# Encoder trunk on one core: score products of 128 rows, scores ahead of a group's first transposes, weights loaded a phase early

## What is computed

```python
h = rmsnorm(x, norm_g)
proj = h @ w_in        # g_q g_k g_v g_lr z_a d_q d_k d_v z_b c_q z_c gate_in
o_a = gla_branch(g_q, g_k, g_v, g_lr, w2, b2, g_norm) * silu(z_a)
o_b = diff_attention(d_q, d_k, d_v, lam_params, g_norm) * silu(z_b)
o_c = memory_cross_attention(c_q, mem, ...) * silu(z_c)
merged = sum_i sigmoid(gate_in[i]) * (branch_i @ w_branch[i])
y = rmsnorm(x + merged @ w_out, final_norm_g)
# differential attention, 4 heads, two maps of 64 channels each:
s = einsum('ibhqd,ibhkd->ibhqk', qblk, kh) + bias     # i = 0, 1; bias = -slope * |tq - pos|
p = softmax(s);  a = p[0] - lam * p[1];  o = a @ v;  o = rmsnorm(o, g_norm) * (1 - lambda_init)
```

## Time and profile before

| | |
|---|---|
| median of 3 runs | 3633.05 us (3632.58 to 3635.64) |
| the profiled execution | 3617.7 us |
| its span | 3615.8 us |
| mean granted clock of TensorE | 0.974 of full |
| busy: TensorE, VectorE, ScalarE, GpSimd | 3411.0, 2048.2, 1326.5, 1213.1 us |
| DMA | 559.88 MB, mean 155 GB/s |

### The profile page before, as it was taken

The page is one execution under the profiler, slowest core; times in us unless marked ns, Lnnn a source line. Parts: engine busy times, 40 slices in busy tenths (PEclk is TensorE's granted clock), DMA queues, the critical chain, the costliest instruction groups (busy, mean ns, idle before and its releaser), DMA issues. The chain is left out here.

```text
span 3615.8 us, 46857 instructions
## 1 busy us (share of the span) xinstructions
PE 3411.0 (94%) x16944; PEld 2563.6 (71%) x16944; DVE 2048.2 (57%) x4688; ACT 1326.5 (37%) x2165; POOL 1213.1 (34%) x510
## 2 busy tenths in 40 slices
PE   7999999989999999999989978999999977999998
PEld 5888888867888888888867754545555545788887
DVE  4222222225665465556666768888887745766554
ACT  3111111123333333333322325656666644333332
POOL 2322321433333333333333325666666632100000
PEclk9999999989999999999999988999999989999999
DMA  6544544563454545434358873121211056765662
GB/s 201 177 166 164 184 160 166 175 212 120 124 180 132 170 125 180 132 123 125 125 176 294 269 209 114 50 82 36 82 55 60 21 196 225 263 231 180 214 209 89
DMA packets 320979, 559.88 MB, mean 155 GB/s; under 512 B 35437, under 2 KB 115565, under 8 KB 320750
## 3 DMA queue, kind: packets, MB, share of 16 engines
q1 hardware_dynamic: 269598, 476.50, 40.7%
q10 hardware_dynamic: 51152, 80.38, 6.1%
HBM read 387.28 MB, written 169.50 MB: 154 GB/s over the span
## 5 line engine op out<-in xcount | busy, mean ns | idle before, releaser
L625 POOL TENSOR_TENSOR glaf_w_lo<-glaf_raw,glaf_w_hi 128x1024 fp32r<-128x1024 f32 x140 | 344.6, 2462 | 723.2 <-ACT glaf_w_hi L595 723.2
L642 PE MATMUL glaf_dense_acc<-h_hi,glaf_w_hi 128*128 128x512 f32 x1120 | 451.8, 403 | 10.6 <-POOL glaf_w_lo L625 5.4
L642 PE MATMUL glaf_dense_acc<-h_hi,glaf_w_lo 128*128 128x512 f32 x1120 | 439.1, 392 | 0.0
L642 PE MATMUL glaf_dense_acc<-h_lo,glaf_w_hi 128*128 128x512 f32 x1120 | 438.8, 392 | 0.0
L1615 DVE CUSTOM_DVE_ANT_0 diff_p<-diff_s_ps,diff_table 128x512 f32<-128x512 f32 x544 | 348.4, 686 | 114.4 <-PE diff_s_ps L1484 110.6
L419 POOL TENSOR_TENSOR proj_w_lo<-proj_raw,proj_w_hi 128x1024 fp32r<-128x1024 f32 x84 | 204.4, 2436 | 482.6 <-DVE proj_w_hi L383 482.6
L1443 POOL TENSOR_SCALAR diff_p<-diff_p,diff_ratio 128x1024 f32<-128x1024 f32 (+1 forms) x80 | 269.0, 3362 | 218.4 <-DVE diff_ratio L1635 218.4
L1508 PE MATMUL diff_oT_ps<-diff_aT,diff_v 128*128 128x512 f32 x544 | 292.1, 638 | 4.6 <-ACT diff_aT L1553 4.6
L1559 ACT ACTIVATE diff_p<-diff_p,diff_neg_max 128x2048 f32<-128x2048 f32 (+1 forms) x160 | 278.6, 1742 | 7.7 <-DVE diff_neg_max L1625 7.6
L1011 DVE COPY_PREDICATED glaf_att<-glaf_picked,glaf_att_ps 128x256 f32<-128x256 int32 x280 | 147.2, 526 | 214.9 <-PE glaf_att_ps L778 208.0
L118 PE MATMUL proj_acc<-h_hi,proj_w_hi 128*128 128x512 f32 x672 | 262.8, 391 | 0.0
(11 more groups left out here) (208 smaller groups left out, 7257.6 us busy)
## 6 DMA issues: line engine op xcount, KB each, us to landing
glaf_raw<-in_w_zg SPq DMA_DIRECT2D x140, 512.0 KB, 3.4
proj_raw<-in_w_stream SPq DMA_DIRECT2D x80, 512.0 KB, 3.6
scratch_zg<-glaf_dense_out SPq DMA_DIRECT2D x140, 256.0 KB, 2.5
merge_raw<-in_w_br SPq DMA_DIRECT2D x120, 256.0 KB, 2.9
merge_gate<-scratch_zg SPq DMA_DIRECT2D x120, 256.0 KB, 3.3
scratch_featT<-proj_out ACTq DMA_DIRECT2D x80, 256.0 KB, 2.2
glab_raw<-in_w_zg SPq DMA_DIRECT2D x40, 512.0 KB, 4.9
items_br_hi<-scratch_item_hi SPq DMA_DIRECT2D x60, 256.0 KB, 6.2
```

The costliest lines, as they stand in the source:

```text
L625: pool.tensor_tensor(self.w_lo[:, s], self.raw[:, u % self.RAW], self.w_hi[:, s], ALU.subtract).then_inc(self.lo_split, 1)
L642: done = pe.matmul(self.acc[:, u % self.BANKS], a, x, start=i == 0, stop=i == self.PER - 1)
```

## The change

- *Projection.* Only tile 0 is transposed ahead of unit 0; tile n+1 is transposed between unit n and unit n+1. Unit 0 (`first_product`) runs its 8 high by high products, then 8 with the low half of the tokens, then 8 with the low half of the weights, and waits for each operand where it is first used. Copies and norms on ScalarE and VectorE follow that order, and the work for the next chunk comes two units later.
- *Weights early.* An object `Early` holds four raw buffers that projection and both GLA passes share, with the gate inputs of the first two tiles. At the end of the projection SP loads the first four weights of the forward pass, at the end of the forward pass those of the backward pass. `Dense` has four raw buffers instead of two. In the same way the cross-attention loads the first four branch weights of the merge.
- *High weights first.* Unit 0 of `Dense` runs its 16 products with `w_hi` first and its 8 with `w_lo` last. The backward pass runs these 16 ahead of its first tile. ScalarE's first copy stands ahead of its table load in both passes, and three copies do in the merge.
- *Backward pass.* SP stores tile n-2 ahead of the gate transfers of the slot.
- *Differential attention.* A score chunk is four 128-row products: keys are held once, high above low, and queries as high above high (`q_high`) and low above zero (`q_low`). Key loads are 4 DMAs instead of 5, query loads 6 instead of 5. In a turn whose transposes open a group (`o.quarter == 0`), the first two score chunks come ahead of the transposes.
- *Cross-attention.* The first memory keys are loaded by ScalarE's queue, and the rest of the first queries ahead of the values.

```diff
+            sp.wait_ge(stored[narrow_units[0] % OUTS], 16 * (narrow_units[0] // OUTS + 1))
+            early.load_gates(sp, narrowT, w2)
+            sp.wait_ge(lo_split, len(pieces))
+            early.load_w(sp, 0, w_zg, FORWARD_UNITS)
...
+            high(0)
             square(1)
-            high(0)
             high_resident(2)
             high_resident(3)
             square(2)
...
             high_resident(5)
-            square(3)
...
                 evacuate(u)
-                if c == 0 and at < 2:
-                    high(2 + at)
+                if c == 0 and at < TT - 1:
+                    high(1 + at)
+                    if at == 0:
+                        square(3)
                     high_resident(6 + at)
-                    if at:
-                        high_resident(8)
-                if at == 2:
+                if at == (TT if c == 0 else 2):
                     store_h(c)
...
             norm(0)
+            low(0)
             norm(1)
-            for n in range(TT):
+            for n in range(1, TT):
+                if n + 1 < TT:
+                    norm(n + 1)
                 low(n)
-                if n + 2 < TT:
...
+            def first_product():
+                tok = slice(0, P)
+                pe.wait_ge(hi_ready, 1)
+                pe.wait_ge(hi_resident, COLS)
+                for k in range(KT):
+                    pe.matmul(acc[:, 0], h_hi[:, 0, k, tok], wv_hi[:, 0, k], start=k == 0, stop=False)
+                pe.wait_ge(lo_ready, 1)
+                for k in range(KT):
+                    pe.matmul(acc[:, 0], h_lo[:, 0, k, tok], wv_hi[:, 0, k], start=False, stop=False)
+                pe.wait_ge(lo_split, COLS)
+                for k in range(KT):
+                    done = pe.matmul(acc[:, 0], h_hi[:, 0, k, tok], wv_lo[:, 0, k], start=False, stop=k == KT - 1)
+                done.then_inc(unit_done, 1)
...
             pe.wait_ge(ident_in, 16)
             transpose(0)
-            transpose(1)
             for u, (kind, c, i, t) in enumerate(units):
                 at = u - first_unit[c]
-                product(u)
-                if c == 0 and at < 2:
-                    transpose(2 + at)
-                j, r = divmod(at, 6)
-                if c < NC and j < TT and r == 2:
+                if u:
+                    product(u)
+                else:
+                    first_product()
+                if c == 0 and at < TT - 1:
+                    transpose(1 + at)
+                j, r = next_chunk(c, at)
+                if c < NC and 0 <= j < TT and r == 2:
```

The weights of the passes and of the merge, and the order of a pass's first unit:

```diff
+    RAW, WEIGHTS, OUTS, BANKS, PER = Early.RAW, 3, 2, 2, 3 * KT
...
-        if u >= self.RAW:
-            sp.wait_ge(self.lo_split, u - self.RAW + 1)
+        sp.wait_ge(self.lo_split, u - self.RAW + 1)
         sp.dma_start(self.raw[:, u % self.RAW], self.dram[2][self.place(u)[1]]).then_inc(self.w_in[u % self.RAW], 16)
...
     def begin_transfers(self, sp):
-        self.load_w(sp, 1)
         for index in range(self.held, self.buffers):
             self.load_h(sp, index)
-        self.load_w(sp, 2)
-        self.load_w(sp, 3)
...
-            self.load_w(sp, u + self.WEIGHTS + 1)
+            self.load_w(sp, u + self.RAW)
...
+    def products_until(self, pe, count):
+        high = 2 * KT
+        while self.emitted < count:
             u, i = divmod(self.emitted, self.PER)
-            k, part = divmod(i, 3)
+            if u:
+                k, part = divmod(i, 3)
+            else:
+                k, part = divmod(i, 2) if i < high else (i - high, 2)
...
             if i == 0:
-                pe.wait_ge(self.lo_split, u + 1)
+                if u:
+                    pe.wait_ge(self.lo_split, u + 1)
+                else:
+                    pe.wait_ge(self.hi_split, 1)
...
+            if u == 0 and i == high:
+                pe.wait_ge(self.lo_split, 1)
...
-            load_gates(0)
-            sp.dma_start(decay_w[:, :], w2).then_inc(decay_in, 16)
-            dense.load_w(sp, 0)
             sp.dma_start(sums_raw, sums_dram).then_inc(sums_in, 16)
...
+            sp.wait_ge(dense.lo_split, dense.count)
+            early.load_w(sp, 1, w_zg, BACKWARD_UNITS)
...
+            dense.high(act, 0)
             act.preload_act_table_set("natural_log_exp_and_others")
...
-            dense.begin_copies(act)
+            for u in range(1, dense.WEIGHTS):
+                dense.high(act, u)
...
-            dense.load_w(sp, 0)
             load_tile(0)
...
-            dense.begin_transfers(sp)
             load_z(0)
...
                 if n + 2 < N:
                     load_tile(n + 2)
+                if n >= 2:
+                    store(n - 2)
                 dense.transfers(sp, 2 * n)
                 dense.transfers(sp, 2 * n + 1)
-                if n >= 2:
-                    store(n - 2)
                 if n + 1 < N:
...
+            dense.products_until(pe, 2 * KT)
             for n in range(N):
...
+            dense.high(act, 0)
             act.preload_act_table(ACT.Sigmoid)
```

The differential attention, the cross-attention and the merge:

```diff
+                    for half, dram, first_block in ((0, featT, DK_BLOCK), (1, featT_lo, DK_BLOCK - DQ_BLOCK)):
+                        sp.dma_start(k[HD * half:HD * (half + 1), s, i].bitcast(FP32), dram[first_block + h, HD * i:HD * (i + 1), cols]).then_inc(k_in[s], 16)
...
+                    rows_of, tok = slice(HD * i, HD * (i + 1)), slice(t0, t0 + CH)
+                    for half in range(2):
+                        sp.dma_start(q_high[HD * half:HD * (half + 1), b, i].bitcast(FP32), featT[DQ_BLOCK + h, rows_of, tok]).then_inc(q_in[b], 16)
+                    sp.dma_start(q_low[0:HD, b, i].bitcast(FP32), featT_lo[h, rows_of, tok]).then_inc(q_in[b], 16)
...
+            pool.wait_ge(ones_ready, 1)
+            pool.memset(q_low[HD:, :, :, :].bitcast(FP32), 0.0).then_inc(ones_ready, 1)
...
                 for i in range(2):
-                    pe.matmul(s_ps[:, chunk % 2, i], q_both[:, b, i, cols], k_both[:, key % KS, i], start=True, stop=False)
-                for i in range(2):
-                    r = slice(HD * i, HD * (i + 1))
-                    done = pe.matmul(s_ps[:, chunk % 2, i], q_high[r, b, cols], k_low[r, key % KS], start=False, stop=True)
+                    pe.matmul(s_ps[:, chunk % 2, i], q_high[:, b, i, cols], k[:, key % KS, i], start=True, stop=False)
+                    done = pe.matmul(s_ps[:, chunk % 2, i], q_low[:, b, i, cols], k[:, key % KS, i], start=False, stop=True)
                 done.then_inc(scores_done, 1)
...
+                opens = ku and o.quarter == 0
+                if opens:
+                    for c in range(min(2, nu)):
+                        scores(n, c)
                 for c in range(2):
                     if c < ku:
                         transposes(o, c)
-                    if c < nu:
+                    if c < nu and not opens:
                         scores(n, c)
...
+            load_q(0, 0, P, q_first_in)
+            load_q(0, P, CH, q_in[0])
             load_memory(0)
-            load_q(0, P, CH)
             load_memory(1)
             load_z(0)
...
             items.load(sp, 0, 2 * H)
+            items.load_w(sp)
...
+            act.dma_start(kT[:, 0], kT_dram[:, :, 0:N_MEM].rearrange("h p s -> p h s")).then_inc(kT_in[0], 16)
...
+    def load_w(self, sp):
+        for u in range(self.RAW):
+            sp.dma_start(self.raw[:, u], self.w_br[u % 3 * KT + u // 3]).then_inc(self.w_in[u], 16)
...
-            for u in range(RAW):
-                load_w(u)
...
-            act.preload_act_table(ACT.Sigmoid)
...
             for u in range(AHEAD):
                 high(u)
+            act.preload_act_table(ACT.Sigmoid)
```

148 lines of the change are left out of this document (79 added, 69 removed).

## The result

The changed kernel takes 3538.65 us (median of 4 runs, 3537.74 to 3541.32), the kernel before 3633.39 beside it: ratio 0.9748, 95% interval 0.9727 to 0.9769. That is 95 us less; 83 were forecast. The profiled executions stand 3617.7 to 3538.0, 80 us, against a sum of 81.6. So the total of the sum held, and what it was carried over to moved: the 15 us between the kernel before's profile and its median were no constant. In three later rounds of measurements the kernel before had medians of 3631, 3624 and 3624, by which the gain would be 85 to 93.

The account below looks back on a forecast made before the run. TensorE, busy 94%, was taken as the bound. Gains summed to 81.6 us off the profiled 3617.7, giving 3536; carrying over the median's 15.35 us gave 3551, stated as 3550 us, own range 3537 to 3563, wider range 3526 to 3574.

Parts of the forecast that it names:

- Score chunk: Attention: four 128-row products save 0.06 us in each of 256 long chunks, 15 us (10 to 20).
- Loads: Changes of head: one key DMA fewer per chunk, one more for queries, 2 us; the attention's starting wait stays.
- Openings and short heads: Attention: scores ahead of transposes fill 14 long openings at 1.9 us each, 27 us; short heads gain 13 us.
- first rival: Attention: VectorE becomes the bound, long groups end near 40.4 us instead of 38.7, 3574 us; chance 0.13.
- Projection: Start of the projection: product 0 starts earlier, three stalls of about 2.8 us follow; +1 us (-6 to +4).
- Starts of passes: Early weights and high-half products first: forward pass gains 8.4 us (5 to 9), backward pass 6.5 (3.5 to 8).
- Backward stalls: Backward pass: five stalls of 13.9 us follow h loads on the same queue and stay; 1 us (-8 to +25).
- third rival: Backward pass: deeper buffers and earlier stores end the stalls and half-clock stretches, 25 us, 3525 us; chance 0.09.
- End of the backward pass and start of the attention: ScalarE waited 4.78 us for a store, now issued earlier: 3.4 us (0 to 4).
- Cross-attention: First memory keys on another queue; the 12.0 us wait is mostly the phase's own start: 1.5 us (0 to 4).
- Rivals 2, 4 and 5: Chunk doesn't shrink, 3565 or 3619 (0.05, 0.01); preloads land no sooner, 3568 (0.05); clock falls to 0.85, 3673 (0.02).
- clock rival: Attention: with openings filled, TensorE's granted clock falls to 0.85, 123 us more, 3673 us; chance 0.02.

Follow-up runs that it names:

- run 4: The changed kernel with the old score chunk (two 128-row and two 64-row products) and its old tiles and loads: 3562.93 us.
- run 6: The changed kernel with GpSimd's sum of the far half waiting, in one turn per group, for that group's norm steps: 3516.72 us.
- run 3: The changed kernel with the projection's old order of transposes, copies and norms: 3535.65 us.
- run 7: The changed kernel with the steps of the inverse square root in the projection's norms reading one tensor each: 3536.32 us.
- run 9: The changed kernel with the backward pass's load of the next z ahead of the 16 loads of h: 3522.93 us.
- runs 1 and 2: The kernel before, unchanged, profiled twice more: 3621.49 and 3628.04 us.

## Why the prediction was right or wrong

The forecast of 3550 was 11 above the result and in its own range. The mechanisms behind most terms were at work, but several terms had the wrong size, and they cancelled: that the sum and the profiles differ by only 1.9 us is in part luck.

- *Score chunk.* The term failed in its size: 16 x 0.06 = 0.96 us a long group, where the products are worth 2.3 (run 4 against run 6). The chunk itself measured 0.06, but I read it only up to the next instruction's start, and the values products behind it were slow by 0.1 too. In the earlier trace rows the chunk was followed by transposes, where only 0.05 of this can be seen.
- *Loads.* The 2 us for one key DMA fewer were too few: the changes of head gained 5.3. And the wait at the attention's start does not stay because ten DMAs are issued before and after: with the old loads back, run 4 has 18.8 us there, the changed kernel 16.5.
- *Openings and short heads.* The hole went as forecast, group by group, and the stretch with the short heads gained 13.8 against 13. An opening is worth 1.6 us a group on top of the old products, and 0.6 on top of the new ones, forecast 1.9.
- *The first rival, in part.* A group should take 38.7 by the sum. With 2.3 for the products in place of 0.96 it would be near 37.4, run 6 has 37.69, and the changed kernel 39.28: the first rival took back 1.6 us per long group, 22 in all. Its mechanism was named (VectorE late at an opening), its price was 1.7, and I gave it 0.13 because of 34.17 us busy. It isn't VectorE's work that counts there, but a step that GpSimd holds up. The same collision was in the earlier trace rows, read for the projection only.
- *Projection.* +1 forecast, -4.7 measured (3 to 4 by run 3), inside the bounds given. The +1 did not follow from its own terms, 7 gained, 8 given back and most of a wait of 5.27 gone, which is nearer +4. Product 0 started at 16.88 as said, and the waits in front of products 1 to 3 were what was said, 8.4 idle in three. Two steps failed. The next tile's transposes came at 26.52, 2.45 us idle behind product 0, since its norm was held up four times instead of three (run 7, without that, is 2.3 us faster). And the half clock behind the waits was not in the sum: products 1 and 2 took 8.27 and 7.17 us, where 24 products at 0.227 are 5.45.
- *Starts of passes.* Forward, 11.4 against 8.4: the gap to the first gate product fell from 15.0 to 5.5 us, a bit more than forecast, and the pass's first stall from 5.6 to 4.5, which wasn't. Backward, 12.2 in the two traces and about 9 over all of them, against 7.5: TensorE's gap between the passes fell from 12.4 to 6.2, 16 products ran before the first tile, and those behind it ran at full clock, as the sum had it.
- *Backward stalls.* Forecast to stay, and they stayed (13.9 and 14.1 us), for the reason given: run 9 shows it. The third rival is out for the change. Run 9, which ends somewhat under half of the waits and all of the falls of the clock, gained 16 of the rival's 25.
- *End of the backward pass and start of the attention.* Forecast 3.4; TensorE's gap there fell from 20.5 to 16.5. By run 4, 2.2 of these 4.0 go with the loads of keys and queries, so the earlier stores gave at most about 1.8.
- *Cross-attention.* The step that failed is the other queue: the wait for the first keys is 12.37 in place of 12.0, on ScalarE's queue as on SyncE's. Whether the phase gained or lost is within what unchanged code scatters by.
- *From the profile to the median.* I carried 15.35 over, and the changed kernel's median is 0.65 above its profile. These 14.7 us, less the 1.9 by which the sum was too high and the rounding from 3551 to 3550, are the 11 between 3550 and 3538.65. The difference was the kernel before's own scatter; by runs 1 and 2 much of it is openings at half clock, which the change removed. That the executions near 3633 are made so is inferred, not seen.
- *Rivals 2, 4 and 5.* All out: full products alternate at 0.23, products start 1.1 to 1.5 us behind a phase's first instruction, and the long group's clock is 1.00. The clock rival had the wrong sign: a filled opening keeps the clock up.

## What to carry to other kernels

Read the price of a matmul form up to where the next group runs at its own rate again, not to the start of its first instruction. When a short VectorE step takes as long as a GpSimd instruction beside it, look at the two side by side: it can bind a stretch in which VectorE is busy 90% of the time (35.31 of 39.26 us), and a wait on GpSimd's side or another form of the step takes it away. Before carrying a profile's distance to the median into a forecast, ask which stretch makes it, since a change may remove just that.
